# A decoder layer of four mixers: S5's read-out in two calls of four column groups, LSTM row maxima ahead of RWKV's third level

## The reference, cut to what matters

```python
h = rms_norm(x, norm_pre_mix);  proj = h @ w_in            # four parts of the columns
y = concat(s5(u), mlstm(p_ml), rwkv7(p_rw), moba(p_mb));   y = group_norm(y) @ w_out
x = x + rms_norm(y);  x = x + rms_norm(cross_attention(rms_norm(x), rms_norm(mem)))
x = x + rms_norm(swiglu(rms_norm(x)))

# S5: 16 groups of 64 complex states, 16 channels each
xs = scan(a * state + B u)                                  # diagonal, over 256 steps
y  = einsum('blgp,ghp->blgh', xs_re, c_re) - einsum('blgp,ghp->blgh', xs_im, c_im)
z  = gelu(y + d * u);  out = z * sigmoid(z @ w_glu + b_glu)

# mLSTM weights need, per head, a running row maximum of the gates (m) before exp
# RWKV-7: state = state * w + (state k') (k' a) + v k, written as a triangular solve per chunk
```

## Time and profile before

| | us |
|---|---|
| median of 3 runs | 490.19 (489.18 to 490.41) |
| profiled execution, span from first to last instruction | 488.3 |
| median less span | 1.9 |
| PE, DVE, ACT, POOL busy | 477.2, 379.2, 258.0, 155.1 |
| mean granted share of PE's clock | 0.994 |

### The profile page before, as it was taken

How to read it: one execution, slowest core, us unless ns; L and a number is a source line. 1 busy time by engine, 2 the same in 40 slices (tenths; PEclk the granted TensorE clock), 3 DMA queues, 4 the chain that set the end, 5 groups by cost and what they waited for, 6 DMA issues and landing times.

```text
span 488.3 us, 8840 instructions
## 1 busy us (share of the span) xinstructions
PE 477.2 (98%) x3650; PEld 427.3 (88%) x3650; DVE 379.2 (78%) x472; ACT 258.0 (53%) x420; POOL 155.1 (32%) x93
## 2 busy tenths in 40 slices
PE   8999999998999999999999999999999999999995
PEld 6999798987888877889998887999999999988884
DVE  3898999998789887787555648899999999952234
ACT  5678884425332347679456656544444444344342
POOL 0005417892375700000000000633334444333550
PEclk9999999998999999999999999999999999999999
DMA  7875329222201226274623622465455554555502
GB/s 267 342 296 186 139 89 343 88 89 82 93 23 66 88 87 258 87 254 130 263 91 137 241 94 87 173 216 182 184 197 199 189 173 172 173 182 213 208 1 87
DMA packets 12700, 78.95 MB, mean 162 GB/s; under 512 B 1487, under 2 KB 2164, under 8 KB 4084
## 3 DMA queue, kind: packets, MB, share of 16 engines
q1 hardware_dynamic: 12660, 78.39, 44.2%
HBM read 77.33 MB, written 1.84 MB: 162 GB/s over the span
## 4 chain that ended last, share of the span: by engine, by line
PE 70%; DVE 5%; issue 1%; ACT 1%; POOL 0%; DVEq 0%
PE bank L395 69%; ACT arena L1391 1%; DVE arena L1953 1%; DVE arena L1820 0%; DVE arena L2022 0%; DVE arena L1819 0%; DVE wm_rest L376 0%; PE bank L933 0%; PE bank L902 0%; DVE h_rest L1884 0%; DVE arena L1973 0%; PE bank L608 0%; POOL arena L1108 0%; DVE kx L1893 0%; DVE small L2004 0%
## 5 line engine op out<-in xcount | busy, mean ns | idle before, releaser
L376 POOL TENSOR_TENSOR w_rest<-ring,w_high 128x1024 fp32r<-128x1024 f32 x20 | 48.5, 2426 | 194.6 <-ACT w_high L370 194.6
L370 ACT ACTIVATE w_high<-ring 128x1024 fp32r<-128x1024 f32 x63 | 66.3, 1060 | 76.7 <-PE bank L395 76.6
L395 PE MATMUL bank<-h_high,w_high 128*128 128x256 f32 x368 | 99.8, 283 | 0.0
L395 PE MATMUL bank<-h_rest,w_high 128*128 128x256 f32 x344 | 97.3, 283 | 0.0
L395 PE MATMUL bank<-h_high,w_rest 128*128 128x256 f32 x320 | 90.6, 283 | 0.0
L376 DVE TENSOR_TENSOR w_rest<-ring,w_high 128x1024 fp32r<-128x1024 f32 x38 | 48.5, 1283 | 28.9 <-ACT w_high L370 28.8
L395 PEld LDWEIGHTS bank<-h_high,w_high 128*128 128x128 f32 x368 | 69.1, 192 | 0.5 <-issue 0.4
L395 PEld LDWEIGHTS bank<-h_rest,w_high 128*128 128x128 f32 x344 | 66.0, 192 | 0.0
L395 PEld LDWEIGHTS bank<-h_high,w_rest 128*128 128x128 f32 x320 | 61.4, 192 | 0.0
L395 PE MATMUL bank<-arena 64*64 64x64 f32 (+8 forms) x794 | 51.6, 254 | 1.6 <-POOL arena L1074 1.1
L395 PEld LDWEIGHTS bank<-arena 64*64 64x64 f32 (+4 forms) x794 | 42.5, 144 | 11.5 <-issue 4.1
(11 more groups left out here) (353 smaller groups left out, 1197.1 us busy)
## 6 DMA issues: line engine op xcount, KB each, us to landing
ring<-weights SPq DMA_DIRECT2D x49, 1024.0 KB, 4.8
third_slot<-weights SPq DMA_DIRECT2D x15, 1024.0 KB, 4.8
gain<-gains SPq DMA_DIRECT2D x3, 512.0 KB, 5.7
cst<-consts SPq DMA_DIRECT2D x1, 1216.0 KB, 8.6
par<-params SPq DMA_DIRECT2D x1, 1168.0 KB, 10.3
kx<-x_t SPq DMA_DIRECT2D x2, 512.0 KB, 5.7
ring<-weights SPq DMA_DIRECT2D x2, 512.0 KB, 6.7
vx<-mem_t SPq DMA_DIRECT2D x1, 1024.0 KB, 9.6
```

The lines of the kernel that those rows point to most:

```text
L370: nc.scalar.activation(split_half(i)[0], raw_half(i), ACT.Copy).then_inc(S["w_high"], 1)
L376: e.tensor_tensor(rest_, raw_half(i), high.bitcast(F32), ALU.subtract).then_inc(rest_done(i)[0], 1)
L395: return nc.tensor.matmul(out_, lhsT, rhs, start=start, stop=stop, skip_group_check=True)
```

## The change

The read-out becomes `s5_out(j, 3)`, j = 0, 1, with 16 matmuls each, the four column groups in turn inside each of the four products. A second buffer for the rotated products lies in `vx`, where the memory lies until its rest is made; `rotate_back(q)` writes buffer q % 2 and waits only for the first read-out, from q = 2 on. The first read-out stands where the second stood, the second where the fourth stood. The LSTM's transposes and row maxima go ahead of `level_p(3)`, ACT's copy of the transposes ahead of its LSTM exponential and `level_evac(3)`. The first half of `wkv(3)` goes ahead of `solve_u(0)`. The read-out is the same 32 matmuls in all.

```diff
--- before.py
+++ after.py
@@ -170,7 +170,8 @@
         (cos_, sin_, bu_, t1_, t2_, pr_, s5u_), at = carve(at, [2048, 2048, 1024, 512, 512, 2048, 512])
         sq_x, sq_m = v3(pr_, T), v3(arena[:, at - 512 - 2048 - 2048:at - 512 - 2048], T)
         cos, sin, t1, t2, s5u = (v3(a, T) for a in (cos_, sin_, t1_, t2_, s5u_))
-        bu, pr = v4(bu_, 2, T), v4(pr_, 2, T)
+        bu = v4(bu_, 2, T)
+        prs = [v4(pr_, 2, T), v4(flat(vx), 2, T)]
         (raw_cv, E_, c2n_), at = carve(at, [4 * 259 + 1024, 4 * 384, 256])
         cv = v3(raw_cv[:, 1036:2060], T)
         mlo, mlv = v3(G.rearrange("p a b -> p (a b)"), T), v3(Gp.rearrange("p a b -> p (a b)"), 256)
@@ -511,15 +512,15 @@
                     last = mm(o[:, e * T:(e + 1) * T], v3(prm(w), P)[r, j, :], s5u[r, j, :])
                 last.then_inc(full[b], 1)
 
-            def s5_out(q, b):
-
-                o = pe_open(pe, "s5_y", b) if q == 0 else bank[b]
-                pe.wait_ge(S["rotated_back"], q + 1)
+            def s5_out(j, b):
+
+                o = bank[b] if j else pe_open(pe, "s5_y", b)
+                pe.wait_ge(S["rotated_back"], 2 * j + 2)
                 for n, (w, x) in enumerate(((c_re, 0), (c_nre, 1), (c_im, 2), (c_im, 3))):
-                    for i in (2 * q, 2 * q + 1):
-                        y = o[32 * (i % 4):32 * (i % 4) + 32, (i // 4) * T:(i // 4 + 1) * T]
-                        last = mm(y, w[:, i, :], pr[:, x, i % 2, :], n == 0, n == 3)
-                last.then_inc(full[b] if q == 3 else S["s5_out_used"], 1)
+                    for g in range(4):
+                        last = mm(o[32 * g:32 * g + 32, j * T:(j + 1) * T], w[:, 4 * j + g, :],
+                                  prs[g // 2][:, x, g % 2, :], n == 0, n == 3)
+                last.then_inc(full[b] if j else S["s5_out_used"], 1)
 
             def level_p(n, c, b):
 
@@ -750,10 +751,6 @@
             split_channel_major(10, "mb_k", 0, h_split)
             level_x(2, 0)
             level_x(2, 1)
-            s5_out(0, 3)
-
-            level_p(3, 0, 4)
-            level_p(3, 1, 6)
             o = v3(pe_open(pe, "g_col", 2)[:, 0:8], 4)
             pe.wait_ge(S["ml_rows"], 1)
             for c in range(NC):
@@ -772,6 +769,8 @@
 
             for h in range(NH):
                 max_row(h)
+            level_p(3, 0, 4)
+            level_p(3, 1, 6)
             split_values(11, "mb_v", 0, h_split)
             level_x(3, 0)
             level_x(3, 1)
@@ -785,7 +784,7 @@
             wkv(0, 1, (1,))
             level_x(4, 0)
             level_x(4, 1)
-            s5_out(1, 3)
+            s5_out(0, 3)
 
             ml_qk(2, 2)
             ml_qk(3, 0)
@@ -817,11 +816,9 @@
             mb_scores(0, 7)
             mb_scores(1, 0)
             mb_scores(2, 2)
-            s5_out(2, 3)
-
             mb_scores(3, 5)
+            wkv(3, 1, (0,))
             solve_u(0, 4)
-            wkv(3, 1, (0,))
             o = pe_open(pe, "S0", 4)
             moved(pe, "U0")
             moved(pe, "rw_bkt")
@@ -834,7 +831,7 @@
             o = pe_open(pe, "bonus", 7)
             pe.wait_ge(S["rw_bonus"], 1)
             mm(o[:, :], const("pair_ones"), flat(bon)).then_inc(full[7], 1)
-            s5_out(3, 3)
+            s5_out(1, 3)
             wkv(3, 1, (1,))
             moved(pe, "S0")
             solve_r(1, 6)
@@ -1113,10 +1110,10 @@
                 pool.wait_ge(S["scanned"], q + 1)
                 if q == 1:
                     pool.wait_ge(S["h_rest"], 4)
-                if q > 0:
-                    pool.wait_ge(S["s5_out_used"], q)
+                if q > 1:
+                    pool.wait_ge(S["s5_out_used"], 1)
                 for x, (a_, b_) in enumerate(((cq, t1), (sq, t2), (cq, t2), (sq, t1))):
-                    last = g.tensor_tensor(pr[:, x], a_, b_, ALU.mult)
+                    last = g.tensor_tensor(prs[q % 2][:, x], a_, b_, ALU.mult)
                 last.then_inc(S["rotated_back"], 1)
 
             def level_mask(n):
@@ -1343,11 +1340,11 @@
             level_evac(2)
             highs(H_MID + 5)
             highs(H_MID + 6)
+            o = wait_full(act, "g_col")
+            a.activation(gcol, o[:, 0:8], ACT.Copy).then_inc(free_of("g_col"), 1)
             act.wait_ge(S["ml_rows"], 3)
             a.activation(rows[4][0:NH, :], rows[4][0:NH, :], ACT.Exp).then_inc(S["ml_em"], 1)
             level_evac(3)
-            o = wait_full(act, "g_col")
-            a.activation(gcol, o[:, 0:8], ACT.Copy).then_inc(free_of("g_col"), 1)
             highs(H_WKV + 1)
             wait_full(act, "mb_v")
             for k in range(KD):
```

## The result

| | before | after |
|---|---|---|
| median of the runs, us (22 runs each) | 489.6 | 491.04 |
| profiled execution, us | 490.19 | 490.27 |
| its span, us | 488.3 | 488.5 |
| the PE start that opens the last stretch, values_low(0), us | 172.20 | 172.31 |

The ratio after to before is 1.0029, with a 95% interval of 1.0017 to 1.0041: slower, by about as much as can be told from no change. The forecast was +2.47 us on 490.19; measured were +1.4 us on 489.6. The 490.19 was the median of three runs, and later runs of the same kernel lie 0.6 lower. Medians here are of all executions, while ratios leave out single ones far above the rest (779 us once in the kernel before) and compare with executions of the kernel before that were taken beside each experiment (medians 489.3 to 489.6 us), so a ratio isn't the quotient of two medians given here.

The account below looks back on a forecast made before the run. PE, busy 98%, was taken as the bound except where the chain runs through POOL and DVE (to 115.78) or DVE and ACT (145.2 to 172.20). Terms 0 + 0 + 0.78 + 1.69 = +2.5 us on 490.19: 492.6, range 489.6 to 494.6.

Parts of the forecast that it names:

- 1.85 in the sum: Each new read-out call: 32 passes, four at a time, 8 steps, taking 1.85 us like an old call.
- rival 2: Read-out: only two matmuls run at a time; +2.9 us, 493.1, with the fall up to 494.5; chance 0.11.
- rival 4: Read-out: weight loads not hidden behind matmuls on the same rows; +1.1 us, 493.7; chance 0.03.
- rival 5: Whole kernel: the two dropped calls' time comes back in full, 3.7 us, giving 486.5; chance 0.05.
- The first stage: 0: First call gone, maxima ahead of level 3: MoBA values 1.5 us earlier, all lost at wkv(0); term 0.
- the 0 taken for the clock at the first wait: At wkv(0), PE's wait 3.25 us instead of 1.74; clock effect between -1.7 and +0.75, taken as 0.
- The swap's first term, U0 late: Around wkv(3,0): PE waits about 1.95 us for bank 1, U0's copy comes late; +0.78 us (0.3 to 1.3).
- the clock term, +1.69: After the new stop ahead of wkv(3,0): clock falls to half near 158.9, U0 another 1.69 us late; ends 0 and 1.7.
- rival 1: At the new stop ahead of wkv(3,0): U0 late but no clock fall; +0.8 us, 491.0; chance 0.28.

Follow-up runs that it names:

- with the keys early: Changed kernel with DVE's mem_keys(2) moved ahead of scan(3), PE's order as in the change: 490.07 us, 1.0013.
- The two fillers of that stop: Changed kernel plus zero matmuls ahead of wkv(3,0): four, with seven more ahead of wkv(0), 490.76 us, 1.0027; three there alone, 490.78 us, 1.0036.
- two moves on DVE and ACT: Kernel before, with DVE's mem_keys(3) ahead of S5's square and ACT's next weight half ahead of S5's exponential: 487.81 us, 0.9969.
- With both stops filled: Changed kernel plus matmuls of zeros in PE's long stops, 7 ahead of wkv(0) and 4 ahead of wkv(3,0): 490.76 us, 1.0027.

## Why the prediction was wrong

**By the three parts.** With the two-call read-out, the four arrangements make a square (ratio to before):

| | swap undone | swap made |
|---|---|---|
| maxima behind level 3 | 1.0026 | 1.0058 |
| maxima ahead of level 3 | 1.0006 | 1.0029 |

The swap costs 0.0023 to 0.0032 in either row, and 0.0024 in the kernel before (the four were not taken at one time, and each difference is good to about 0.002). The maxima ahead give back 0.0020 to 0.0029 of the 0.0026 that the read-out leaves in its wake. So the net result is, within that, the swap's price.

**The read-out: right.** Four at once in 1.87 us, against 1.85 in the sum; rivals 2 and 4 fall, and rival 5 with the sign of the result. Rival 4's sentence of the Trainium skill (TensorE: Matmul & The Clock Gate, "The mechanism"), that a load hides only behind matmuls of another row group, doesn't hold for these tiles: the fours start every 0.22 us, the time of a pass, with all of their loads on the same rows. (The section also speaks of loads into a background buffer of weights; no run here shows whether that is how.) The same page's "Measured speedup vs the span model", by which I estimated 2.2 us a call, is also above the trace: from 1.85 for two groups to 1.87 for four, the array does twice the work in the same time.

**The first stage: 0 was right as a net, for another reason than given.** Level 3 started at 102.18, which is the 101.84 of the working in an execution that is 0.3 us later, and the time was lost ahead of wkv(0) as said. What the working left out is that this place is filled for the clock's sake too. Leave it empty and the read-out alone costs 0.0026; the maxima fill it. It was also not foreseen that a fall may then come at 104, in the slack, in place of 117: the wait at wkv(0) was 1.71, not 3.25, and PE's stretch behind it took 27.87 us in place of 29.34. So the 0 taken for the clock at the first wait wasn't what this execution had either: it had 0.67 us less at the keys. With the swap undone, and with the keys early, a fall stands near 116 again.

**The swap's first term, U0 late: right, in size too.** The wait for L1890 (2.19 against 1.95), the copy that waits for PE, S0 behind it, values_low(0) behind the keys: all are in the profile as drawn. The copy starts 4.38 us after wkv(3,0) (156.74 to 161.12), where the working had 4.39 (157.42 to 161.81). It is only 0.09 late against the earlier trace rows because the keys came 0.67 us early in this execution; less that, it is late by 0.76, where the sum had 0.78. Swapped in the kernel before, where the read-out stands ahead of wkv(3,0), it is 1.75 late.

**The step that failed is the clock term, +1.69.** "I take 1.69, since the row nearest in length fell" made a fall that was seen once, in one execution, a certainty for every execution of the changed kernel. It is real where it comes (1.50 in the profile with the maxima put back) and it did not come in the profile of the change, after a longer stop. The whole price of the swap is 1.1 us (0.3 to 1.9), where the sum had 2.47, and the swap alone costs as much with no stop and no fall beside it. The likeliest forecast should have carried it as a share: 0.78 with a fall in some executions, which is between the forecast and rival 1.

How often it falls there isn't shown, since only the mean granted clock is known of executions that were not profiled. One fall of 3.4 us lowers that mean by 3.4 x 0.5 / 488, 0.0035. Of the change's 22 executions, the 12 at 0.994 or 0.995 average 490.0 us and the 8 at 0.988, two falls more, 492.5; with the swap undone the 5 at 0.989 or 0.990 average 490.3. That fits a stop that falls now and then and then costs about two us more than the same falls elsewhere, but it is argued and not shown. The two fillers of that stop leave it open.

**The base.** The forecast time was a further 0.6 us too high because it stood on the median of three runs. Rival 1's 491.0 meets the measured 491.04 by that accident: its +0.8 was 0.6 too small, as the forecast's +2.47 was 1.0 too large.

## What to carry to other kernels

A fall of the clock that is seen in one profile is one draw: price a new stop by a share of a fall, and ask for each fall whether it lies on the path or in slack, since some 3.4 us at half clock were free at 104 and cost PE 1.5 us at 117 (29.34 against 27.87) and at 158 (4.56 against 3.06). Matmuls that are off the path may be holding the clock up: taking out a read-out that cost nothing left a stop of 2 us, and that cost 1.3 us until something else filled it. And read an engine's slack at a join from more than one execution before calling the other engine's order worthless; two moves on DVE and ACT, priced at 0 to 0.4 us by one profile, were worth 0.3%, 1.5 us.

## What the runs showed of the hardware that was not expected

- Four fp32 column tiles of 128x32 on the same 128 rows run together at the pace of two: 32 passes of 256 columns in 1.87 us, where 16 took 1.85.
- The clock can fall with next to no stop of PE ahead. In the kernel before with the two moves, PE was busy 5.82 of the 6.00 us ahead of 105.1 and then was granted 0.50 for 3.3 us; with the maxima ahead alone it was busy all of 100.7 to 104.1 and fell at 104.3. Both times the work ahead was the read-out, the maxima, on 4 rows, and blocks of 64x64. The kernel before runs the same work up to there as it does with the two moves, and its profile has no fall at 105 but one at 117. With both stops filled it fell at 145.9 behind 2.80 us in which PE was busy throughout. A stop of 2.19 us was followed by no fall at all.
- A fall can last longer than one of 3.4 us: behind the stop at level 3 the clock stayed at 0.50 for some 10 us.
